# Value rows of the last 128 tokens summed on VectorE, and value tiles collected four at a time in PSUM

## The chip, the cores and the metric

The kernel runs on one core of a Trainium2 chip. The metric is the device time of one execution in microseconds; the median of three runs is given. Engines are named as in the profile: PE (TensorE matmul), PEld (its weight load), DVE (VectorE), ACT (ScalarE), POOL (GpSimd), SP (SyncE).

## The reference, cut to what matters

One transformer layer (differential attention, a pooling branch, gates) is followed by a mixture of 16,384 one-row experts. The change lies in the last part, the sum over value rows:

```python
def peer_block(h, w_q, sub_keys, u, v):
    ...                                        # 8 heads x 16 chosen experts = 128 for each token
    act = jax.nn.gelu(jnp.einsum('nd,nhkd->nhk', h, u[experts]), approximate=False)
    return jnp.einsum('nhk,nhkd->nd', (gate * act).astype(h.dtype), v[experts])
```

There are 576 tokens (512 of the prompt, 64 of the samples), `v` is 16,384 x 2048 in float32 (128 MB), and each token needs 128 rows of it. The result is added to `h` and normalized.

## The kernel before

Everything up to the value part stays as it is, but for small preparations. The value part treats three sets of tokens in two ways.

**Tokens 0 to 383 (`TV`), dense.** All of V is multiplied with a weight matrix that is zero where a token did not choose an expert. V is cut into 128 tiles of 128 experts x 2048 columns. SP loads a tile into one of two buffers `v_raw` (`load_v`, L566), ACT casts it to `v_hi` (`value_high`, L1116), DVE subtracts to get `v_lo` (`value_low`, L1712). Gates times activations are loaded by SP (`load_weights`, L569), multiplied by DVE (`weigh`, L1718), and split by ACT and DVE into `wx_hi` and `wx_lo` (L1123, L1724). PE works on pairs of tiles (loop at L2274): for each of 16 column blocks `d` it issues three products (hi·hi, hi·lo, lo·hi) for each of two tiles into one PSUM bank, six matmuls of 128x128 by 384 columns, and DVE adds the bank to `main` (`take_sum`, L1730). Four banks are used in turn: before block d, PE waits until DVE has taken block d-4 (L2286). There are 64 pairs and 1,024 `take_sum`.

**Tokens 384 to 575, gathered.** For these 192 tokens POOL gathers each token's 128 rows, with expert slots on the partitions (`gather_rows`, L748; 1 MB each). Four tokens make a batch; there are 48. PE multiplies a batch with a 128x32 weight tile per token, 16 float32 matmuls of 512 columns (`expert_sums`, L2231), before block d=4 of pairs 3 to 40 (32 batches) and 43 to 61 (16 batches). `e_rows` has eight buffers, two batches. The activations of tokens 384 to 447 (`N_CELL` = 64) are gathered too, one element per partition (`gather_cells`, L739); those of the last 128 tokens come from dot products on DVE (L1689).

**Order.** Each engine's program is written out by hand and runs in order; semaphores join them. DVE's order in a pair is `take_sum` for each d, with `value_low` after d=3 and 6, `weigh` after 8 and 9, `weight_low` after 11 and 12 (L1755 to L1771). POOL's loop (L780) waits for a batch's matmuls, weighs the batch two ahead, gathers its rows, and then gathers the cells four ahead. All gathers go out on POOL's own DMA queue (q0), all loads of SP on another (q1), and both run on the same 16 DMA engines.

Of the kernel before, what the change touches and what calls it, by code (L numbers as in the profile page):

```python
# [26 lines left out]
P = 128  # L27
# [45 lines left out]
N_CELL = TU - TV  # L73
U_RING = 3
# [31 lines left out]
def tokens(tb):  # L106
    return P if tb < TB - 1 else NS


def hybrid_step(nc, x_prompt, x_sample, cache_k, cache_v, state_pool, page_table, norm1_g, w_in, b_gate,  # L110
# [4 lines left out]
    with ctx:  # L115
# [55 lines left out]
        e_act = Region(masks_at, iota_at)("e_act", [P, N_SP])  # L171
        e_slot = Region(iota_at + P * 4, A_X)("e_slot", [P, PK], U32)
        e_cell = Region(iota_at + P * 4, A_X)("e_cell", [P, N_CELL], U32)
        e_row = Region(pages_at, A_X)("e_row", [P, N_SP], U32)
# [94 lines left out]
        v_raw = [r(f"v_raw{s}", [P, D]) for s in range(2)]  # L269
        wx_hi = [r(f"wx_hi{s}", [P, TV], R) for s in range(4)]  # L270
        wx_lo = [r(f"wx_lo{s}", [P, TV], R) for s in range(4)]
        e_rows = [r(f"e_rows{s}", [P, D]) for s in (5, 6)]
        g_back = [None, r("g_back1", [P, N_HALF, 2, GB // 2])]
        e_w = [r(f"e_w{s}", [P, COLS, QR]) for s in range(2)]
        r = Region(A_X, END)
        e_rows = [r("e_rows0", [P, D])] + e_rows
# [3 lines left out]
        e_gate = r("e_gate", [P, N_SP])  # L280
        r("spare", [P, N_SP])
        e_rows = e_rows[0:1] + [r(f"e_rows{s}", [P, D]) for s in range(1, 5)] + e_rows[1:]
        e_rows.append(Region(A_MAIN - D * 4, A_MAIN)("e_rows7", [P, D]))
        first_x = [Region(A_X + 2 * T * 4, back_at), Region(back_at + 4 * TV * 4 + 2 * N_SP * 4 + 3 * D * 4, END - 4096)]
        first_x = [[r(f"first_x{i}{j}", [P, TV], R) for j in range(2)] for i, r in enumerate(first_x)]
        first_hi = [nc.alloc_sbuf_tensor_at(f"first_hi{m}", [P, D], R, offset=BASE + back_at + 4 * TV * 4 + 2 * N_SP * 4 + 2 * m * D * 4) for m in range(2)]
        first_lo = nc.alloc_sbuf_tensor_at("first_lo", [P, D], R, offset=BASE + back_at + 4 * TV * 4 + 2 * N_SP * 4 + D * 4)
# [117 lines left out]
        V_RAW = [U_RAW[s] + 16 * NQ * N_U // 2 for s in range(2)]  # L405
        h_mm, H_MM, h_ev, H_EV = xr_mm, TB, xr_ev, 2 * TB
        dot_done, DOT = x_scaled, 2 * TB
        u_row_in, e_in = kp_in[0:U_RING], (vp_in, kp_in)
        U_IN = 16 * DB * PAGES // K_RING
        E_IN = [[U_IN] * COLS, [U_IN + 16 * len(range(j, N_SU, U_RING)) * (j < U_RING) for j in range(COLS)]]  # L410
        CELLS_IN = [16 * (2 + 8 + (8 if s < 2 else 0)) for s in range(4)]

        def batch_tokens(b):

            k = 0 if b < SP_BLOCKS[1][0] else 1
            first, nb, _ = SP_BLOCKS[k]
            return [COLS * first + nb * j + b - first for j in range(COLS)], b - first

        def value_parts(n):

            return first_hi[n] if n < 2 else v_hi[n % 4], first_lo if n == 0 else v_lo[n % 4]

        def weight_parts(n):

            return first_x[n] if n < 2 else (wx_hi[n % 4], wx_lo[n % 4])
# [63 lines left out]
        def _(sp):  # L489
# [76 lines left out]
            def load_v(n):  # L566
                sp.dma_start(v_raw[n % 2][:, :], v_tiles[:, n, :]).then_inc(raw_in[n % 2], 16)

            def load_weights(n):  # L569
                sp.dma_start(a_back[n % 2][:, :], gelu_dram[n][:, 0:TV]).then_inc(ag_in[n % 2], 16)  # L570
                if n % 2 == 0:
                    sp.dma_start(g_back[n // 2 % 2][:, :, :, :], gmat_dram[:, n // 2]).then_inc(ag_in[0], 16)
# [6 lines left out]
            sp.wait_ge(top_done, N_PQ + 5)  # L579
            for s in range(2):  # L580
                sp.wait_ge(a_out[s], 16)
                load_weights(s)
            sp.wait_ge(u_turn, 2 * N_U - 2)
            load_v(0)
            store_gelu(N_U - 3)
            sp.wait_ge(u_turn, 2 * N_U)
            load_v(1)
# [5 lines left out]
            for p in range(1, N_PAIR):  # L593
                for n in (2 * p, 2 * p + 1):
                    sp.wait_ge(v_lod, n - 1)
                    load_v(n)
                for s in range(2):
                    sp.wait_ge(a_out[s], 32 if p == 1 else 16 * N_U // 2)
                for n in (2 * p, 2 * p + 1):
                    sp.wait_ge(wx_lod, n - 1)  # L600
                    load_weights(n)
# [10 lines left out]
        def _(pool):  # L612
# [126 lines left out]
            def gather_cells(b):  # L739

                for t in batch_tokens(b)[0]:
                    if t >= N_CELL:
                        break
                    pool.indirect_dma_start(out=e_act[:, t:t + 1], out_offset=None, in_=gelu_cells,
                                            in_offset=bass.IndirectOffsetOnAxis(ap=e_cell[:, t:t + 1], axis=0)
                                            ).then_inc(back_in[b % 4], 16)

            def gather_rows(b):  # L748

                for j, t in enumerate(batch_tokens(b)[0]):  # L750
                    pool.indirect_dma_start(out=e_rows[b % 2 * COLS + j][:, :], out_offset=None, in_=v_rows,
                                            in_offset=bass.IndirectOffsetOnAxis(ap=e_row[:, t:t + 1], axis=0)
                                            ).then_inc(e_in[b % 2][j], 16)

            def weigh(b):

                ts_, c = batch_tokens(b)
                at = slice(ts_[0], ts_[-1] + 1, ts_[1] - ts_[0])
                if b < SP_BLOCKS[1][0]:
                    pool.wait_ge(back_in[b % 4], CELLS_IN[b % 4] + 32 * (b // 4 + 1))  # L760
                if b >= 2:
                    _, last = batch_tokens(b - 2)
                    g.memset(e_w[b % 2][:, :, last], 0.0).then_inc(e_wval, 1)
# [3 lines left out]
                g.tensor_tensor(e_w[b % 2][:, :, c], e_act[:, at], e_gate[:, at], ALU.mult).then_inc(e_wval, 1)  # L767

            pool.wait_ge(top_done, N_PQ + 5)
# [3 lines left out]
            for b in range(2):  # L773
                gather_rows(b)
            for b in range(4):
                gather_cells(b)
            pool.wait_ge(h_ev, H_EV + 6)
# [17 lines left out]
        def _(act):  # L795
# [320 lines left out]
            def value_high(n):  # L1116

                act.wait_ge(raw_in[n % 2], 16 * (n // 2 + 1) + V_RAW[n % 2])
                if n >= 4:
                    act.wait_ge(acc_ps, (n // 2 - 1) * KD)  # L1120
                a.copy(value_parts(n)[0][:, :], v_raw[n % 2][:, :]).then_inc(v_hid, 1)
# [1205 lines left out]
```

## Time and profile before

| | us |
|---|---|
| median of three runs | 4501.45 (4498.28 to 4503.62) |
| the profiled execution | 4504.14 |
| its span | 4502.4 |
| PE busy in the span | 4378.3 (97%) |
| DVE busy | 2908.6 (65%) |
| ACT busy | 1211.7 (27%) |
| POOL busy | 700.7 (16%) |
| value part: first and last matmul of L2260 | 3204.04 to about 4458.5 |

The profile sums instructions over one execution, so shares of busy time are means over stages with different limits. Durations of matmuls overlap: 337 ns is one matmul from start to end, while the next begins 0.17 us after it. Times "at" a point count from the start of the span.

### The profile page before, as it was taken

What the parts mean: (1) busy time and instruction counts of PE and PEld (TensorE: products, weight loads), DVE (VectorE), ACT (ScalarE), POOL (GpSimd) and SP (SyncE); (2) the same over time, 40 slices, a digit from 0 to 9 for tenths busy, and PEclk for the clock granted to TensorE, in tenths of its full rate; (3) what the DMA queues carried; (4) which work ended last, traced back from release to release, by engine and by line L of the source; (5) the groups of instructions that cost most, each with busy time, mean ns of one, the idle gap of its engine ahead of it and who ended that gap; (6) DMA issues with size and microseconds to landing.
All of it is one profiled execution on the core that took longest, in us unless ns stands there. A gap on an engine that the chain in (4) does not pass through costs nothing.

```text
span 4502.4 us, 69308 instructions
## 1 busy us (share of the span) xinstructions
PE 4378.3 (97%) x29448; PEld 4054.6 (90%) x29448; DVE 2908.6 (65%) x4670; ACT 1211.7 (27%) x1490; POOL 700.7 (16%) x744
## 2 busy tenths in 40 slices
PE   8999999999999989999999999999999999999997
PEld 7999889998899979888899999999988888898887
DVE  3232552322434366899998989898677777777777
ACT  3221442322212121223322222222222222222223
POOL 1010002331000000000111111111133333312220
PEclk9999999999999989999999999999999999999998
DMA  6333235775344533355899999999888888878872
GB/s 197 110 105 96 78 97 191 239 245 175 107 126 126 155 78 74 90 126 124 229 285 285 277 285 282 275 291 274 303 329 327 325 316 320 328 279 327 328 303 95
DMA packets 571731, 968.42 MB, mean 215 GB/s; under 512 B 140817, under 2 KB 402961, under 8 KB 512792
## 3 DMA queue, kind: packets, MB, share of 16 engines
q1 hardware_dynamic: 490128, 519.33, 40.7%
q0 software_dynamic: 75776, 434.18, 25.3%
q10 hardware_dynamic: 5520, 10.49, 0.8%
q8 instruction: 233, 3.82, 0.3%
q14 instruction: 74, 0.61, 0.0%
HBM read 873.63 MB, written 85.75 MB: 213 GB/s over the span
## 4 chain that ended last, share of the span: by engine, by line
PE 87%; DVE 9%; issue 1%; ACT 1%; DMA 1%; SPq 0%; ACTq 0%; DVEq 0%
PE pair L1838 28%; PE pair L2260 23%; PE pair L2179 21%; PE quad L2241 4%; PE quad L1838 2%; PE pair L2214 2%; DVE w_lo L1560 2%; PE pair L1802 1%; PE quad L1802 1%; DVE turned L1555 1%; PE quad L2009 1%; ACT w_hi L819 1%; PE pair L1874 1%; PE quad L2052 1%; DVE ts L1576 1%
## 5 line engine op out<-in xcount | busy, mean ns | idle before, releaser
L2179 PE MATMUL pair<-act_hi,w_hi 128*128 128x448 f32 x2048 | 758.8, 371 | 14.8 <-DVE w_lo L1560 14.8
L1733 DVE TENSOR_TENSOR main<-pair,main 128x384 f32<-128x384 f32 x1024 | 552.9, 553 | 323.3 <-PE pair L2260 322.8
L2179 PE MATMUL pair<-act_lo,w_hi 128*128 128x448 f32 x2048 | 749.7, 366 | 0.0
L2179 PE MATMUL pair<-act_hi,w_lo 128*128 128x448 f32 x2048 | 749.6, 366 | 0.0
L1838 PE MATMUL pair<-act_hi,w_hi 128*128 128x288 f32 x3264 | 719.4, 302 | 29.3 <-DVE act_lo L1265 12.3
L1205 DVE TENSOR_TENSOR w_lo<-w_raw,w_hi 128x2048 fp32r<-128x2048 f32 x103 | 236.1, 2293 | 747.0 <-ACT w_hi L819 747.0
L1838 PE MATMUL pair<-act_hi,w_lo 128*128 128x288 f32 x3264 | 702.8, 297 | 0.0
L1838 PE MATMUL pair<-act_lo,w_hi 128*128 128x288 f32 x3264 | 701.2, 297 | 0.0
L2260 PE MATMUL pair<-wx_hi,v_hi 128*128 128x384 f32 x2016 | 679.3, 337 | 1.6 <-DVE main L1733 1.6
L2260 PE MATMUL pair<-wx_hi,v_lo 128*128 128x384 f32 x2016 | 674.2, 334 | 0.0
L2260 PE MATMUL pair<-wx_lo,v_hi 128*128 128x384 f32 x2016 | 673.4, 334 | 0.0
L1838 PEld LDWEIGHTS pair<-act_hi,w_hi 128*128 128x128 f32 x3264 | 526.5, 190 | 67.7 <-issue 61.5
L1838 PEld LDWEIGHTS pair<-act_lo,w_hi 128*128 128x128 f32 x3264 | 528.8, 190 | 0.0
L1838 PEld LDWEIGHTS pair<-act_hi,w_lo 128*128 128x128 f32 x3264 | 528.7, 190 | 0.0
L819 ACT CAST w_hi<-w_raw 128x2048 fp32r<-128x2048 f32 x112 | 213.5, 1907 | 829.7 <-PE pair L1838 728.3
L2179 PEld LDWEIGHTS pair<-act_hi,w_hi 128*128 128x128 f32 x2048 | 385.8, 188 | 48.8 <-DVE w_lo L1560 15.0
L2260 PEld LDWEIGHTS pair<-wx_hi,v_hi 128*128 128x128 f32 x2016 | 378.3, 188 | 42.2 <-issue 40.2
L2179 PEld LDWEIGHTS pair<-act_hi,w_lo 128*128 128x128 f32 x2048 | 385.6, 188 | 31.1
L2179 PEld LDWEIGHTS pair<-act_lo,w_hi 128*128 128x128 f32 x2048 | 385.9, 188 | 29.7
L2260 PEld LDWEIGHTS pair<-wx_lo,v_hi 128*128 128x128 f32 x2016 | 378.4, 188 | 0.0
L2260 PEld LDWEIGHTS pair<-wx_hi,v_lo 128*128 128x128 f32 x2016 | 378.3, 188 | 0.0
L1560 DVE TENSOR_TENSOR w_lo<-turned,w_hi 128x1024 fp32r<-128x1024 f32 x256 | 309.0, 1207 | 103.9 <-ACT w_hi L1067 101.9
(323 smaller groups left out, 5206.8 us busy)
## 6 DMA issues: line engine op xcount, KB each, us to landing
w_raw<-in_peer_u_dram SPq DMA_DIRECT2D x512, 256.0 KB, 5.6
v_raw<-in_peer_v_dram SPq DMA_DIRECT2D x128, 1024.0 KB, 5.7
w_raw<-in_w_in_dram SPq DMA_DIRECT2D x64, 1024.0 KB, 6.8
gelu_dram<-tmp SPq DMA_DIRECT2D x128, 224.0 KB, 7.4
gmat_dram<-gmat SPq DMA_DIRECT2D x48, 512.0 KB, 11.2
a_back<-gelu_dram SPq DMA_DIRECT2D x128, 192.0 KB, 8.3
g_back<-gmat_dram SPq DMA_DIRECT2D x64, 384.0 KB, 9.5
w_raw<-in_w_out_dram SPq DMA_DIRECT2D x16, 1024.0 KB, 7.0
```

Source lines behind the costliest of these rows:

```text
L819: a.copy(w_hi[g % 2][:, :, :], w_raw[g % 2][:, :, :]).then_inc(hi_done, 1)
L1205: v.tensor_sub(w_lo[g % 2][:, :, :], w_raw[g % 2][:, :, :], w_hi[g % 2][:, :, :].bitcast(F)).then_inc(lo_done, 1)
L1555: v.transpose(turned[i][:, :, :].rearrange("p k (e c) -> p e k c", c=QR), raw[:, :, 8 * i:8 * i + 8, :]).then_inc(u_turn, 1)
L1560: v.tensor_sub(w_lo[s][:, 8 * i:8 * i + 8, :], turned[i][:, :, :], w_hi[s][:, 8 * i:8 * i + 8, :].bitcast(F)).then_inc(u_lo, 1)
L1576: link(*[v.max(out=ts[0:w, h, at:at + 8], in_=cand[0:w, h, :]) for h in range(PH)])
L1733: v.tensor_add(main[:, d, 0:TV], bank(d), main[:, d, 0:TV]).then_inc(acc_done, 1)
L1802: return nc.tensor.transpose(out, in_, ident[0:n, 0:n])
L1838: op = m_(pair[out][:, hf, 0:TH], w[:, k, :], x[:, k, hf * TH:(hf + 1) * TH], start=(starts and k == ks[0] and i == 0), stop=(ends and k = ...
L2179: op = m_(pair[0][:, n % 2, 0:TU], w[n % 2][:, k, :], x[:, k, 0:TU], start=(k == 0 and i == 0), stop=(k == KD - 1 and i == 2))
L2214: op = m_(pair[1][:, g % 2, n * PK:(n + 1) * PK], one_i[g % 2][:, n, :], gate_j[g % 2][:, n, :], start=True, stop=True)
L2241: op = m_(pair[2 + c // 2][quadrant(j), c % 2, :], e_w[b % 2][:, j, :], e_rows[b % 2 * COLS + j][:, c * 512:(c + 1) * 512], start=first, s ...
L2260: op = m_(bank(d), w[:, c], x[:, :], start=(start and t == terms[0]), stop=(stop and t == terms[-1]))
```

## The change

It has three parts.

1. **The last 128 tokens (448 to 575) leave PE.** Token on the partition, slot by slot: `gather_slot(i)` brings the i-th chosen row of all 128 tokens (1 MB, two buffers `s_rows`), and `add_slot(i)` on DVE does `s_sum = s_rows * weight + s_sum` over 2048 columns. The 128 sums are placed by the table `SUMS`: after d = 4, 7, 12 and 15 of groups 1 to 31, and after d=6 in groups 5, 12, 19 and 26. In the last group PE turns `s_sum` with 16 transposes and DVE adds the result to `main`.
2. **16 batches remain on PE** (tokens 384 to 447), before d=4 of groups 2, 3, 5, 6, 8, 9 ... 23, 24. `e_rows` has four buffers instead of eight, so the rows of batch b+1 are gathered after the matmuls of batch b. POOL then gathers the cells of batch b+2 and weighs that batch at once.
3. **PSUM collects four tiles.** The tiles are grouped (0, 1), then fours, and last (126, 127): 33 groups, 528 `take_sum`. V is loaded, cast and subtracted in halves of 1024 columns (three raw buffers of 512 KB, named by `V_HALF`). The high half (d 8 to 15) of a group's tiles is prepared in d 1 to 5 of the group itself, the low half of the next group's tiles in d 9 to 13. `wx_hi` and `wx_lo` have eight buffers.

The core of the diff (buffer addresses, names and the start of the stage are left out):

```diff
-SP_BLOCKS = ((0, 32, 3), (32, 16, 43))
-N_BATCH = sum(nb for _, nb, _ in SP_BLOCKS)
-SP_PAIR = {pair + i * 6 // 5: first + i for first, nb, pair in SP_BLOCKS for i in range(nb)}
-SP_LAST = {pair + (nb - 1) * 6 // 5: k for k, (_, nb, pair) in enumerate(SP_BLOCKS)}
+SP_N = 16
+SP_GROUP = [2 + 3 * b // 2 for b in range(SP_N)]
+SP_LAST = SP_GROUP[-1]
+V_GROUPS = [(0, 1)] + [tuple(range(n, min(n + 4, N_U))) for n in range(2, N_U, 4)]
+N_VG = len(V_GROUPS)
+V_GROUP = {n: g for g, ns in enumerate(V_GROUPS) for n in ns}
+V_HALF = [(0, 0), (0, 1), (1, 0), (1, 1)] + [(n, h) for ns in V_GROUPS[1:] for h in range(2) for n in ns]
+V_AT = {x: i for i, x in enumerate(V_HALF)}
+V_RAWS = 3
+SUMS = sorted([(g, d) for g in range(1, N_VG - 1) for d in (4, 7, 12, 15)] + [(g, 6) for g in (5, 12, 19, 26)])
+SUM_AT = {x: i for i, x in enumerate(SUMS)}
+BATCH_AFTER = {min(i for i, x in enumerate(SUMS) if x > (SP_GROUP[b], 4)) + 2: b for b in range(SP_N - 1)}
...
-            return [COLS * first + nb * j + b - first for j in range(COLS)], b - first
+            return [SP_N * j + b for j in range(COLS)]
...
+            def load_v(i):
+                if i >= V_RAWS:
+                    sp.wait_ge(v_lod, i - V_RAWS + 1)
+                n, half = V_HALF[i]
+                sp.dma_start(v_raw[i % V_RAWS][:, :], v_tiles[:, n, half * D // 2:(half + 1) * D // 2]).then_inc(v_in[i % V_RAWS], 16)
+
+            def load_weights(k):
+                if k:
+                    sp.wait_ge(wx_val, 2 * k)
+                for s in range(2):
+                    sp.wait_ge(a_out[s], 16 * (k + 1) if k < 2 else 16 * N_U // 2)
+                sp.dma_start(a_back[0][:, :], gelu_dram[2 * k][:, 0:TV]).then_inc(ag_in[0], 16)
+                sp.dma_start(g_back[k % 2][:, :, :, :], gmat_dram[:, k]).then_inc(ag_in[0], 16)
+                sp.dma_start(a_back[1][:, :], gelu_dram[2 * k + 1][:, 0:TV]).then_inc(ag_in[1], 16)
...
+            for g in range(1, N_VG):
+                if 2 + 2 * g < N_PAIR:
+                    load_weights(2 + 2 * g)
+                for n in V_GROUPS[g]:
+                    if V_AT[n, 1] + V_RAWS < len(V_HALF):
+                        load_v(V_AT[n, 1] + V_RAWS)
+                if 3 + 2 * g < N_PAIR:
+                    load_weights(3 + 2 * g)
+                for n in V_GROUPS[g + 1] if g + 1 < N_VG else ():
+                    if V_AT[n, 0] + V_RAWS < len(V_HALF):
+                        load_v(V_AT[n, 0] + V_RAWS)
```

```diff
+
+            def gather_slot(i):
+
+                pool.indirect_dma_start(out=s_rows[i % 2][:, :], out_offset=None, in_=v_rows,
+                                        in_offset=bass.IndirectOffsetOnAxis(ap=e_slot[:, i:i + 1], axis=0)
+                                        ).then_inc(s_in[i % 2], 16)
 
             def weigh(b):
+                pool.wait_ge(back_in[b % 4], CELLS_IN[b % 4] + 16 * COLS * (b // 4 + 1))
...
+            for i in range(2):
+                gather_slot(i)
+            gather_cells(0)
+            gather_rows(0)
+            gather_cells(1)
             for b in range(2):
                 weigh(b)
-            for b in range(N_BATCH):
-                pool.wait_ge(e_mm, b + 1)
-                if b + 2 < N_BATCH:
-                    weigh(b + 2)
-                    if b + 2 == SP_BLOCKS[0][1] + 1:
-                        pool.wait_ge(e_turned, 2)
-                    gather_rows(b + 2)
-                if b + 4 < N_BATCH:
-                    gather_cells(b + 4)
+            for i in range(2, PK + 2):
+                if i < PK:
+                    pool.wait_ge(s_done, S_DONE + i - 1)
+                    gather_slot(i)
+                if i in BATCH_AFTER:
+                    b = BATCH_AFTER[i]
+                    pool.wait_ge(e_mm, b + 1)
+                    gather_rows(b + 1)
+                    if b + 2 < SP_N:
+                        gather_cells(b + 2)
+                        weigh(b + 2)
```

```diff
+            def value_high(i):
+
+                n, half = V_HALF[i]
+                g, c = V_GROUP[n], slice(half * D // 2, (half + 1) * D // 2)
+                act.wait_ge(v_in[i % V_RAWS], 16 * (i // V_RAWS + 1) + V_IN)
+                if g >= 2:
+                    act.wait_ge(acc_ps, (g - 1) * KD + 8 * (half + 1))
+                a.copy(value_parts(n)[0][:, c], v_raw[i % V_RAWS][:, :]).then_inc(v_hid, 1)
...
+            for g in range(1, N_VG):
+                after = V_GROUPS[g + 1] if g + 1 < N_VG else ()
+                for n in V_GROUPS[g][0:3]:
+                    value_high(V_AT[n, 1])
+                for n in after[0:2]:
+                    weight_high(n)
+                for n in V_GROUPS[g][3:4]:
+                    value_high(V_AT[n, 1])
+                for n in after[0:3]:
+                    value_high(V_AT[n, 0])
+                for n in after[2:4]:
+                    weight_high(n)
+                for n in after[3:4]:
+                    value_high(V_AT[n, 0])
+                if g == SP_LAST:
+                    take_expert_sums()
```

```diff
+            def add_slot(i):
+
+                dve.wait_ge(s_in[i % 2], S_IN[i % 2] + 16 * (i // 2 + 1))
+                if i == 0:
+                    v.tensor_scalar(s_sum[:, :], s_rows[0][:, :], s_act[:, 0:1], None, ALU.mult).then_inc(s_done, 1)
+                else:
+                    dve.wait_ge(s_done, S_DONE + i)
+                    v.scalar_tensor_tensor(s_sum[:, :], s_rows[i % 2][:, :], s_act[:, i:i + 1], s_sum[:, :],
+                                           ALU.mult, ALU.add).then_inc(s_done, 1)
...
+            for g in range(1, N_VG):
+                after = V_GROUPS[g + 1] if g + 1 < N_VG else ()
                 for d in range(KD):
-                    if p == 0 and d == H_EARLY:
-                        dve.wait_ge(hT_back, 32)
-                    if p < N_PAIR - 1 or d < 12:
-                        take_sum(p, d)
-                    if p + 1 < N_PAIR:
-                        if d == 3:
-                            value_low(2 * p + 2)
-                        if d == 6:
-                            value_low(2 * p + 3)
-                        if d in (8, 9):
-                            weigh(2 * p + d - 6)
-                        if d in (11, 12):
-                            weight_low(2 * p + d - 9)
-                    if d == 13 and p - 1 in SP_LAST:
-                        add_expert_sums(SP_LAST[p - 1])
+                    if g < N_VG - 1 or d < 12:
+                        take_sum(g, d)
+                    if d in (0, 8):
+                        for n in after[d // 4:d // 4 + 2]:
+                            weigh(n)
+                    if d in (6, 14):
+                        for n in after[d // 8 * 2:d // 8 * 2 + 2]:
+                            weight_low(n)
+                    if d in (1, 2, 3, 5):
+                        i = (1, 2, 3, 5).index(d)
+                        for n in V_GROUPS[g][i:i + 1]:
+                            value_low(V_AT[n, 1])
+                    if d in (9, 10, 11, 13):
+                        i = (9, 10, 11, 13).index(d)
+                        for n in after[i:i + 1]:
+                            value_low(V_AT[n, 0])
+                    if (g, d) in SUM_AT:
+                        add_slot(SUM_AT[g, d])
+                    if (g, d) == (SP_LAST + 1, 11):
+                        add_expert_sums()
+                    if (g, d) == (N_VG - 1, 5):
+                        add_slot_sums()
```

```diff
-                    pe.wait_ge(e_added, 2)
                 for j in range(COLS):
-                    pe.wait_ge(e_in[b % 2][j], 16 * (b // 2 + 1) + E_IN[b % 2][j])
+                    pe.wait_ge(e_in[j], 16 * (b + 1) + U_IN)
...
+            for g, ns in enumerate(V_GROUPS):
+                if g:
+                    pe.wait_ge(v_lod, V_AT[ns[-1], 0] + 1)
+                    pe.wait_ge(wx_lod, ns[-1] + 1)
+                for d in range(0 if g else 4, KD):
+                    if d == 8:
+                        pe.wait_ge(v_lod, V_AT[ns[-1], 1] + 1)
+                    if d == 4 and g in SP_GROUP:
+                        expert_sums(SP_GROUP.index(g))
+                    if (g, d) == (SP_LAST + 1, 8):
+                        pe.wait_ge(e_taken, 2)
+                        turn_rows(e_rows[0])
+                    if (g, d) == (N_VG - 1, 2):
+                        pe.wait_ge(e_added, 2)
+                        pe.wait_ge(s_done, S_DONE + PK)
+                        turn_rows(s_sum)
+                    pe.wait_ge(acc_done, g * KD + d - 3)
+                    for n in ns:
+                        op = value_terms(d, n, (0, 1, 2), n == ns[0], n == ns[-1])
+                    op.then_inc(acc_ps, 1)
+            pe.wait_ge(acc_done, N_VG * KD)
```

## Rows read from the trace of the kernel before

**Rows 1.** The page, part 1: busy us, share of the span, instructions.
```profile
PE 4378.3 (97%) x29448; PEld 4054.6 (90%) x29448; DVE 2908.6 (65%) x4670; ACT 1211.7 (27%) x1490; POOL 700.7 (16%) x744
```
**Rows 2.** Groups by line, 3300 to 4502 us: busy us, mean ns | idle before.
```profile
L2260 PE MATMUL pair<-wx_hi,v_hi 128*128 128x384 f32 x1891 | 637.2, 337 | 0.0
...
L1733 DVE TENSOR_TENSOR main<-pair,main 128x384 f32<-128x384 f32 x947 | 512.1, 553 | 305.8 <-PE pair L2260 305.3
...
L1121 ACT CAST v_hi<-v_raw 128x2048 fp32r<-128x2048 f32 x116 | 220.4, 1912 | 253.3 <-PE pair L2260 214.1 <-DMA v_raw<-in_peer_v_dram 39.3
L2241 PE MATMUL quad<-e_rows,e_w 128*32 128x512 f32 x1472 | 167.5, 595 | 0.0
...
L1793 DVE SCALAR_TENSOR_TENSOR tmp<-main,gfc,rstd 128x576 f32<-128x576 f32 x16 | 12.6, 818 | 1.9 <-PE quad L1802 1.3
L1784 DVE TENSOR_TENSOR nf_sum<-nf_sum,nf_sq 128x576 f32<-128x576 f32 x15 | 11.3, 756 | 1.3
```
**Rows 3.** Busy time by stretch: PE, PEld, DVE, ACT, POOL, granted clock, DMA share, GB/s.
```profile
3216.00:3226.00 10.00, 10.00 (x51) 10.00 (x50) 8.84 (x15) 1.43 (x5) 0.00 (x0) 0.83 0.83 279
3400.00:3600.00 200.00, 200.00 (x1246) 174.05 (x1246) 144.85 (x220) 48.42 (x40) 70.75 (x72) 1.00 0.86 333
```
**Rows 4.** The chain that ended last, in order of time: start us, us, what.
```profile
3588.01 33.50 PE pair L2260 x192
...
3625.09 16.86 PE pair L2260 x96
...
3645.52 16.86 PE pair L2260 x96
```
**Rows 5.** Timeline of DVE: start us, us, line, operation [idle before].
```profile
3608.98 2.28 DVE L1716 TENSOR_TENSOR v_lo<-v_raw,v_hi 128x2048 fp32r<-128x2048 f32 x1
3611.18 1.01 DVE L1733 TENSOR_TENSOR main<-pair,main 128x384 f32<-128x384 f32 x2
3612.11 0.55 DVE L1722 TENSOR_TENSOR a_back<-a_back,g_back 128x384 f32<-128x384 f32 x1
3612.58 0.55 DVE L1733 TENSOR_TENSOR main<-pair,main 128x384 f32<-128x384 f32 x1
```
**Rows 6.** Timeline of POOL around one batch.
```profile
3625.59 0.96 POOL L751 DMA_INDIRECT e_rows<-in_peer_v_dram,e_row  x1
...
3633.76 0.95 POOL L744 DMA_INDIRECT e_act<-gelu_dram,e_cell  x1 [0.31 <-issue]
```
**Rows 7.** DMA of that batch, 3625.2 to 3645.6 us.
```profile
q0 software_dynamic: 635, 4.20, 53.6%
q1 hardware_dynamic: 706, 2.86, 37.5%
...
e_act<-gelu_dram,e_cell POOLq DMA_INDIRECT x2, 12.1
```
**Rows 8.** Timeline of POOL at the start of the stage.
```profile
3226.49 0.94 POOL L751 DMA_INDIRECT e_rows<-in_peer_v_dram,e_row  x1 [78.34 <-PE pair L2260]
...
3260.19 0.20 POOL L765 MEMSET e_w<- 128x128 f32 x1 [10.05 <-DMA e_act<-gelu_dram,e_cell]
```
**Rows 9.** DMA of 3300 to 4300 us: size, median us from issue to landing.
```profile
v_raw<-in_peer_v_dram SPq DMA_DIRECT2D x101, 1024.0 KB, 5.7
```
**Rows 10.** The tile e_rows over the same stretch.
```profile
DMA to landing us min/median/max: 6.5/8.0/16.8
```
**Rows 11.** Timeline of PE around a wait at the start of the stage.
```profile
3212.84 0.27 PE L1802 MATMUL quad<-ident,e_act 128*128 128x128 f32 x1
3215.57 0.70 PE L2260 MATMUL pair<-first_x,first_hi 128*128 128x384 f32 x2 [2.46 <-DVE main L1733]
3216.07 0.52 PE L2260 MATMUL pair<-first_x,first_lo 128*128 128x384 f32 x1
```

More of the change, by code:

```diff
@@ L73 @@
 N_CELL = TU - TV
+assert len(SUMS) == PK and SP_N * 4 == N_CELL
 U_RING = 3
@@ L268, in hybrid_step @@
         r = Region(A_RING, A_CONST)
[L269 to L272, printed above, removed]
+        v_raw = [r(f"v_raw{s}", [P, D // 2]) for s in range(V_RAWS)]
+        wx_hi = [r(f"wx_hi{s}", [P, TV], R) for s in range(8)]
+        lo_at = r.at - BASE
+        wx_lo = [r(f"wx_lo{s}", [P, TV], R) for s in range(8)]
+        wx = [Region(lo_at + s * TV * 4, A_CONST)(f"wx{s}", [P, TV]) for s in range(8)]
+        e_row3 = r("e_rows3", [P, D])
         g_back = [None, r("g_back1", [P, N_HALF, 2, GB // 2])]
         e_w = [r(f"e_w{s}", [P, COLS, QR]) for s in range(2)]
+        s_sum = Region(A_MAIN - D * 4, A_MAIN)("s_sum", [P, D])
+        first_lo = [None, Region(A_MAIN - D * 4, A_MAIN)("first_lo1", [P, D], R)]
         r = Region(A_X, END)
-        e_rows = [r("e_rows0", [P, D])] + e_rows
+        e_rows = [r("e_rows0", [P, D])]
         back_at = r.at - BASE
@@ L279, in hybrid_step @@
         g_back[0] = r("g_back0", [P, N_HALF, 2, GB // 2])
[L280 to L287, printed above, removed]
+        e_gate = r("e_gate", [P, N_CELL])
+        e_cell = r("e_cell", [P, N_CELL], U32)
+        rows_at = r.at - BASE
+        e_rows += [r(f"e_rows{s}", [P, D]) for s in (1, 2)] + [e_row3]
+        s_rows = [r(f"s_rows{s}", [P, D]) for s in range(2)]
+        r = Region(A_X + 2 * T * 4, back_at)
+        first_x = [[r(f"first_x0{j}", [P, TV], R) for j in range(2)]]
+        first_wx = [Region(A_X + 2 * T * 4 + TV * 4, back_at)("first_wx0", [P, TV])]
+        r = Region(rows_at, END - 4096)
+        first_hi = [r("first_hi0", [P, D], R)]
+        first_lo[0] = r("first_lo0", [P, D], R)
+        first_hi.append(r("first_hi1", [P, D], R))
+        first_wx.append(Region(r.at - BASE + TV * 4, END)("first_wx1", [P, TV]))
+        first_x.append([r(f"first_x1{j}", [P, TV], R) for j in range(2)])
         r = Region(back_at, END)
@@ L592, in _ @@
             sp.wait_ge(a_done, N_U)
[L593 to L601, printed above, removed]
+            load_v(3)
+            load_weights(1)
+            for i in (4, 5, 6):
+                load_v(i)
+            load_weights(2)
+            for i in (7, 8, 9):
+                load_v(i)
+            load_weights(3)
+            load_v(10)
+            for g in range(1, N_VG):
[9 more added lines that the diff above has]
+                        load_v(V_AT[n, 0] + V_RAWS)
             for n in range(4):
@@ L766, in weigh @@
                     pool.wait_ge(e_wval, 2 * b + 1)
[L767 to L769 removed]
+                g.tensor_tensor(e_w[b % 2][:, :, b], e_act[:, b::SP_N], e_gate[:, b::SP_N], ALU.mult).then_inc(e_wval, 1)
+            pool.wait_ge(top_done, N_PQ + 4)
             pool.wait_ge(acc_ps, KD)
@@ L1745, in add_expert_sums, with add_slot_sums @@
                     op.then_inc(e_added, 1)
+            def add_slot_sums():
+                for i in range(2):
+                    dve.wait_ge(e_turned, 2 + i + 1)
+                    ps, ks = turned_x(pair[2 + i], P), slice(8 * i, 8 * i + 8)
+                    v.tensor_add(main[:, ks, T - NS:T], ps[:, :, 0:NS], main[:, ks, T - NS:T])
+                    v.tensor_add(main[:, ks, TU:T - NS], ps[:, :, NS:P], main[:, ks, TU:T - NS]).then_inc(e_added, 1)
             for m in range(2):
```

200 lines of the change are left out of this document (87 added, 113 removed).

## The prediction

> **What bounds the kernel now.** The page's busy shares come first: PE is busy for 97% of the span and DVE for 65% [rows 1]. Shares are means over stages, so the next view is the stretch of the value part: from 3400 to 3600 us PE is busy all the time at the full clock, DVE 72%, ACT 24%, and the 16 DMA engines 86% at 333 GB/s [rows 3]. The groups say with what: the matmuls of L2260 (this row for each of three products), the 32-column float32 matmuls of L2241, and on DVE above all `take_sum` [rows 2]. DVE's idle time before `take_sum` is 305.8 us, 305.3 of it put down to PE [rows 2]: DVE waits for PE, not the reverse. The chain in order of time gives the rhythm: two pairs, one of them with a batch, take 3625.09 - 3588.01 = 37.08 us, and one pair with a batch 3645.52 - 3625.09 = 20.43 us [rows 4]. So a bare pair takes 16.65 us (1.04 per block d) and a batch adds 3.78 us. Only PE is on the chain.
>
> **What the change takes from PE.** The matmuls of the dense part stay as they are; PSUM collects twelve instead of six, so a block lasts 2.08 us and a group of four tiles 33.3 us. Of 48 batches 16 stay: 32 x 3.78 = 121.0 us leave PE. The transposes of the sums are 32 before and after, and one transpose of activations goes; I cost this at nothing.
>
> **Does DVE still fit beside PE?** Durations overlap by a little, so I take distances between starts: `value_low` 2.20 us (3608.98 to 3611.18), a 384-column operation 0.47 us (3612.11 to 3612.58) [rows 5]. Per group of four tiles: 16 `take_sum` 7.5, 8 `weigh` and `weight_low` 3.7, 8 halves of `value_low` at about 1.13 (half the columns, the same start cost) 9.0, and 4 `add_slot`. No row shows that operation at 2048 columns; scalar_tensor_tensor takes 818 ns against 756 for a plain addition at 576 columns [rows 2], so between 2.20 and 2.20 x 818/756 = 2.38; I take 2.2, because the difference looks like a start cost, not one per column: 8.8. The sum is 29.0 us of 33.3. DVE's share rises from 72% to 87% although `take_sum` takes 7.5 instead of 15 us of the same work. It keeps up on average, and `take_sum` may lag by three blocks (6.2 us) before PE waits. But two other deadlines are closer. The last high half of V is subtracted after d=5, and PE needs it before d=8: if `add_slot` at d=4 starts at its planned place, that is ready 1.7 us early. The last `weight_low` of a group comes after d=14 and is ready some 0.4 us before PE's next group. So a late `add_slot` at d=4 costs PE whatever exceeds 1.7 us.
>
> **When are the gathered rows there?** This is the main added cost. In the trace one batch of four rows (4 MB) and two cell gathers goes out from 3625.59; the last cell gather is issued at 3633.76 and lands 12.1 us later, 20.3 us after the first issue [rows 6, 7]. Both queues share the engines then, q0 53.6% and q1 37.5% [rows 7]. At the start of the stage eight rows and eight cell gathers take 3260.19 - 3226.49 = 33.7 us [rows 8]. Hence 3.35 us for each further MB: five rows take about 23.7 us. In the new kernel POOL, at the place of a batch, issues one slot row, four batch rows and four cell gathers and then stands still until the cells have landed, because `weigh(b+2)` follows directly. Behind it, on the same engine, is the gather of the slot row for d=4 of the next group. Before the change the cells had been gathered a batch earlier and nobody waited for them.
>
> Clock of one group g with a batch, from its start: PE ends d=7 at 8 x 2.08 + 3.8 = 20.4; DVE takes it and adds the slot, 23.2; POOL issues there. The cells land at 23.2 + 23.7 = 46.9, POOL gathers the slot at 47.5, and it lands 8.0 later (the median of these gathers [rows 10]) at 55.5. Batches are followed alternately by a group without one (after batches 1, 3 ... 13: seven times) and by a group with one (after batches 0, 2 ... 14: eight times).
> - Followed by none: group g ends at 37.1, DVE wants the slot of d=4 at 48.2. It comes 7.3 late, less 1.7 of room: PE stands 5.6 us. A standing PE also loses clock: after a gap of 2.46 us the next matmuls take 0.52 instead of 0.33 us [rows 11], and the next 10 us ran at a granted 0.83 [rows 3], that is 1.7 us lost. 7 x 7.3 = 51 us. Bounds: POOL free already after 20.3 and a landing in the quickest 6.5 [rows 10] give 0.7 each, 5 us in all. For the slow end SP's own loads count: 5.2 MB of rows and 3.8 MB that SP loads meanwhile (six halves of V and the weights of a pair), at 4.20 + 2.86 MB in 20.4 us [rows 7], are 26 us; with the landing 8.0 that is 9.6 each with the clock, 67 us.
> - Followed by one: the four batch rows, in the same queue, are there at about 46.9; PE wants them at 37.1 + 8.3 = 45.4. It stands 1.5 us, and the slot that follows is about 0.3 late: 8 x 1.8 = 14 us. Bounds: 0 and, with 26 us and the clock, 8 x 5.5 = 44 us.
> - Start of the stage: POOL's first request is six rows and eight cell gathers, 20.3 + 2 x 3.35 = 27 us, then the slot for d=12 of group 1, wanted at 27.7, lands at 27 + 0.6 + 8.0 = 35.6; with 0.5 of room PE stands 7.4, plus clock 1.7. Preparing four half tiles and four weights in the 16.6 us of group 0 may be 2 late. 11 us (0 to 15).
> - Groups 5, 12, 19, 26 place a third sum at d=6. The row for d=7 is gathered only when the sum of d=4 is done and lands 3.5 us late on DVE, of which d=14 still feels about 1.5: 6 us (0 to 14).
> - The loads of V in halves: 1 MB lands in 5.7 us in the median [rows 9]; a half must land in 6.5 us at d=13 (below). Cost 0, up to 10.
>
> **The sum.** 4504.1 (the profiled execution) - 121 + 51 + 14 + 11 + 6 = 4465. The median of the runs is 2.7 us under the profiled execution, so **4462**. With all lower bounds the costs are 5 us (4386 on the median's scale), with all upper ones 150 us (4531).
>
> The landing times carry this, and a rule of the skill gives others. The Trainium skill, DMA: Bandwidth & Descriptors, section "Anatomy of one DMA — SWDGE (gpsimd) path", fits a transfer at 2.0 us plus its bytes over 436 GB/s. By that estimate five rows are there in 14 us, POOL is free long before it is needed, and only the 121 us remain. The trace does not agree where both queues work: 4 MB of rows took 20 us, not 12.
>
> **The rivals.**
> - *The rows are there in time* (chance 0.15). If SP's loads fall in the pauses of q0, five rows could take the time of four, 20.3 us or less, and the landings 6.5: no wait at d=4 exceeds its room. For it: in a batch's period the two queues have 91% between them, so a tenth is free [rows 7]. Against it: the DMA engines are at 86% already [rows 3], the bytes stay the same, and the time shrinks. Costs 5 to 25 us: 4386 to 4405. This is also what the skill's fit above would give.
> - *Slower: the halves of V come late* (chance 0.2). Place: `value_low` after d=13, the last of the next group. Its buffer comes free with the sum after d=9 (22.7 us after the start of a bare group), its load stands behind two weight loads and a `g_back` in q1, ACT casts it (about 1.0, half of the 1.9 that the row L1121 of the groups gives [rows 2]), and the last `weight_low` follows. It must land 6.5 us after issue. A whole tile lands in 5.7 in the median [rows 9], rows of q0 in 8.0 and up to 16.8 [rows 10]. At 9.0, every group is 2.5 us late: 31 x 2.5 = 78 us on top of the 82 above, 4540. From 1.6 us late per group (a landing after 8.1 us) the change is slower than before by more than 9 us. For it: three small buffers instead of two large ones, and busier DMA. Against: a half is half the bytes.
> - *The costs just eat the gain* (chance 0.12): the waits at d=4 at their slow end with the other terms (67 + 44 + 11 + 6 = 128, less 121), 4492 to 4511.
> - *The change doesn't do what it says*: that is excluded for PE, whose 512 matmuls are gone from its program.
>
> **How the numbers follow.** My forecast, waits behind the batch of gathers that cost 30 to 112 us, has 0.53: 4411 to 4492 by its own range. A measurement of this kernel can tell about 0.2%, 9 us, from no change. Forecast and first rival are faster: 0.68. Same: 0.12. Slower: 0.20. The range for 8 in 10 leaves out the quick end of the first rival and the far half of the second: 4398 to 4525.
>
> **What would show it.** Right: L2241 with a third of its instructions; DVE near 87% in the middle of the stage; PE's gaps about 7 us long at d=8 of groups 4, 7, 10 ... 22 with the releaser DVE `v_lo`, before it DVE `s_sum` waiting for the DMA `s_rows`, and POOL's `e_w` waiting for the DMA `e_act`; from group 25 on bare groups of 33.3 us. After each gap a few matmuls at 0.52 us. Wrong: `s_rows` landing without DVE waiting (first rival), or gaps in every group, also after group 25, with `v_raw` as the releaser of ACT (second). If `add_slot` took over 3 us, DVE itself would be the bound, and no landing time would matter.

## The result, and the profile after

| | before | after |
|---|---|---|
| median of four runs, us | 4502.3 | 4559.27 (4553.33 to 4564.21) |
| ratio | | 1.0128, 95% interval 1.011 to 1.0145 |
| span of the profiled execution | 4502.4 | 4556.9 |
| PE busy in it | 4378.3 (97%) | 4298.1 (94%) |

The kernel became 57 us slower; 40 us faster had been forecast. PE did lose the work: L2337, which answers to L2241 of [rows 2], has a third of its instructions. The page's first part:

```profile
PE 4298.1 (94%) x28423; PEld 4058.2 (89%) x28423; DVE 2952.4 (65%) x4428; ACT 1221.2 (27%) x1614; POOL 671.0 (15%) x680
```

Busy time by stretch, in the middle of the value part and after its last batch (columns as in [rows 3], where PE was busy all the time):

```profile
3400.00:3600.00 200.00, 176.28 (x1023) 163.82 (x1022) 141.69 (x169) 46.82 (x57) 57.98 (x52) 0.93 0.80 300
4300.00:4400.00 100.00, 97.08 (x559) 96.49 (x558) 89.76 (x107) 29.19 (x35) 12.28 (x13) 1.00 0.84 298
```
In the middle PE is idle for 12% and has a granted clock of 0.93. DVE is at 71%, far from the 87% forecast, and the DMA engines at 80%, less than before: nothing is full. After the last batch PE is at 97% with the full clock and DVE at 90%, about the list that was added up. So in the steady part of the stage the time is lost where batches are; a smaller loss at the start of the stage comes on top (see "Why the prediction was wrong").

The groups of lines (columns as in [rows 2]):

```profile
L1794 DVE SCALAR_TENSOR_TENSOR s_sum<-s_rows,s_act,s_sum 128x2048 f32<-128x2048 f32 x122 | 285.8, 2343 | 12.6 <-DMA s_rows<-in_peer_v_dram,e_slot 12.6
L1773 DVE TENSOR_TENSOR v_lo<-v_raw,v_hi 128x1024 fp32r<-128x1024 f32 x233 | 283.4, 1216 | 128.3 <-ACT v_hi L1168 128.3
...
L1168 ACT CAST v_hi<-v_raw 128x1024 fp32r<-128x1024 f32 x233 | 240.8, 1050 | 882.0 <-DMA v_raw<-in_peer_v_dram 671.6 <-PE pair L2355 210.1
...
L2337 PE MATMUL quad<-e_rows,e_w 128*32 128x512 f32 x480 | 54.6, 595 | 0.0
```
`add_slot` takes 2343 ns, `value_low` of a half 1216. From start to start they are 2.25 us (3601.86 to 3604.11 on DVE's timeline) and 1.13 (3630.72 to 3631.85), inside what had been set down (2.20 to 2.38, and 1.13). ACT's cast of V, L1168, has 671.6 us of idle time that end with a load of V; the row of L1121 in [rows 2], which answers to it, had 39.3. And the slot rows, which the forecast feared, cost DVE 12.6 us in all.

The chain in order of time shows one gap from end to end (start us, us, what):

```profile
3582.41 8.55 PE pair L2355 x48
...
3595.70 1.14 DVE v_lo L1773
...
3596.86 13.48 DMA v_raw<-in_peer_v_dram
...
3610.36 1.05 ACT v_hi L1168
...
3611.44 1.24 DVE v_lo L1773
...
3614.17 44.52 PE pair L2355 x240
```
PE works until 3590.96. Its next matmul of this chain starts at 3614.17, after: `value_low` of the next group's first tile (3595.70, d=9), which frees a raw buffer; the load into it, 13.48 us; cast; and `value_low` at d=13. Only then come the last `weight_low` and the next group. A chain does not say how long PE stood (it also worked on the rest of its group meanwhile). PE's timeline does, for this place:

```profile
3614.17 0.66 PE L2355 MATMUL pair<-wx_hi,v_hi 128*128 128x384 f32 x1 [6.58 <-issue]
```
and the stretch after it (columns as in [rows 3]):

```profile
3616.00:3618.00 2.00, 2.00 (x8) 2.00 (x7) 0.80 (x1) 1.39 (x2) 1.37 (x3) 0.50 0.22 78
```
It stood 6.58 us, and the granted clock then was 0.50, the lower of its two levels. What that costs is on the chain one gap earlier: the first 48 matmuls of the group (from 3568.66) take 10.18 us, the 48 after its batch 8.55. The view of waits has 22 idle stretches of PE with 124 us, the longest 10.2:

```profile
ACT v_hi L1168 <- DMA v_raw<-in_peer_v_dram: 671.6, 144, 17.4
...
DVE v_lo L1773 <- ACT v_hi L1168: 128.3, 26, 10.4
PE pair L2355 <- issue: 124.1, 22, 10.2
...
DVE s_sum L1794 <- DMA s_rows<-in_peer_v_dram,e_slot: 12.6, 4, 6.4
```
The chain restarts after such gaps at 3442.70, 3488.28 and 3568.66. From the first to the last are three groups with two batches: 125.96 us, where 3 x 33.3 + 2 x 3.78 = 107.5 were due by the prices of [rows 4], so 9.2 us for each of the two gaps between them, its slow clock included. From group 2 to group 24 the chain holds 14 loads of V of 13.3 us or more (13 of them up to 14.9, one 17.1), one for each of POOL's 15 requests but one; at that one, near 3740 us, it goes over a cell gather of 6.60 and a slot row of 9.20 instead, which is the forecast's path.

The two gaps are not the dearest. Measured from `take_sum` of block d=8 to that of the next group on DVE's timeline, the fifteen stretches after a request are 8.8 to 12.4 us over their price (33.3, and 3.78 for a batch in them), 156 us together; the other stretches up to group 31 are over it by 19 us in all.

What happens beside the load is on POOL's timeline:

```profile
3594.07 0.94 POOL L798 DMA_INDIRECT s_rows<-in_peer_v_dram,e_slot  x1 [5.30 <-DVE s_sum L1794]
...
3607.86 0.95 POOL L785 DMA_INDIRECT e_act<-gelu_dram,e_cell  x1 [0.31 <-issue]
3616.45 0.11 POOL L806 MEMSET e_w<- 128x4 f32 x1 [7.64 <-DMA e_act<-gelu_dram,e_cell]
```
Its nine gathers go out from 3594.07; the load of V is issued at 3596.84, into that burst. And the DMA engines do not share evenly. Rows of queues (packets, MB, share of 16 engines), first of the kernel before, 3634.5 to 3638.5, when rows and V (8 KB per partition) were under way:

```profile
q1 hardware_dynamic: 108, 0.88, 52.2%
q0 software_dynamic: 113, 0.82, 48.5%
```
and of the kernel after, 3601 to 3605 us (q1 has weights in pieces of 1.5 and 3 KB):

```profile
q0 software_dynamic: 180, 1.34, 79.5%
q1 hardware_dynamic: 181, 0.36, 22.9%
```
and 3606 to 3613 us (q1 has halves of V, 4 KB per partition):

```profile
q0 software_dynamic: 268, 1.97, 67.4%
q1 hardware_dynamic: 263, 0.98, 35.0%
```
Equal numbers of packets in all three, but bytes 1:1 before and 2:1 or nearly 4:1 after. A packet is one piece of a row here. So in these stretches the queues are served alternately, packet by packet; in others of the same burst the counts differ (154 of q0 and 246 of q1 from 3597 to 3601 us). This agrees with the Trainium skill, DMA: Bandwidth & Descriptors, section "Queues, rings and completion order", by which an engine goes round the queues packet by packet. It gives halves of V 0.14 MB per us beside a burst, where whole tiles had 0.22.

### The profile page after: what moved, and what is told of

It is laid out like the page before. It is cut to its first block, busy times and chain, and to the rows that moved or that the text cites. A ratio compares the mean times of both kernels' runs of the same rounds, so it can differ in the third digit from the quotient of the medians.

```text
span 4556.9 us, 67360 instructions
## 1 busy us (share of the span) xinstructions
PE 4298.1 (94%) x28423; PEld 4058.2 (89%) x28423; DVE 2952.4 (65%) x4428; ACT 1221.2 (27%) x1614; POOL 671.0 (15%) x680
## 4 chain that ended last, share of the span: by engine, by line
PE 77%; DVE 12%; DMA 7%; issue 2%; ACT 2%; SPq 0%; POOL 0%; ACTq 0%; DVEq 0%
PE pair L1937 28%; PE pair L2278 21%; PE pair L2355 16%; DMA v_raw<-in_peer_v_dram 5%; PE quad L1937 2%; PE pair L2313 2%; DVE w_lo L1615 2%; PE pair L1901 1%; PE quad L2337 1%; PE quad L1901 1%; DVE s_sum L1794 1%; DVE turned L1610 1%; DVE v_lo L1773 1%; PE quad L2108 1%; ACT w_hi L864 1%
## 5 line engine op out<-in xcount | busy, mean ns | idle before, releaser
L2355 PE MATMUL pair<-wx_hi,v_hi 128*128 128x384 f32 x2016 | 696.4, 345 | 136.9 <-issue 124.1
L2355 PE MATMUL pair<-wx_lo,v_hi 128*128 128x384 f32 x2016 | 690.0, 342 | 0.0
L2355 PE MATMUL pair<-wx_hi,v_lo 128*128 128x384 f32 x2016 | 689.3, 342 | 0.0
L2355 PEld LDWEIGHTS pair<-wx_hi,v_hi 128*128 128x128 f32 x2016 | 391.6, 194 | 158.2 <-issue 148.7
L1168 ACT CAST v_hi<-v_raw 128x1024 fp32r<-128x1024 f32 x252 | 260.5, 1050 | 937.0 <-DMA v_raw<-in_peer_v_dram 715.5
L1800 DVE TENSOR_TENSOR main<-pair,main 128x384 f32<-128x384 f32 x528 | 291.6, 554 | 187.8 <-PE pair L2355 187.6
L1773 DVE TENSOR_TENSOR v_lo<-v_raw,v_hi 128x1024 fp32r<-128x1024 f32 x252 | 306.5, 1216 | 137.2 <-ACT v_hi L1168 137.2
L2355 PEld LDWEIGHTS pair<-wx_lo,v_hi 128*128 128x128 f32 x2016 | 391.6, 194 | 0.0
## 6 DMA issues: line engine op xcount, KB each, us to landing
gmat_dram<-gmat SPq DMA_DIRECT2D x48, 512.0 KB, 12.4
```

Of the source, the lines that this page charges most:

```text
L1168: a.copy(value_parts(n)[0][:, c], v_raw[i % V_RAWS][:, :]).then_inc(v_hid, 1)
L1773: v.tensor_sub(lo[:, c], v_raw[i % V_RAWS][:, :], hi[:, c].bitcast(F)).then_inc(v_lod, 1)
L1800: v.tensor_add(main[:, d, 0:TV], bank(d), main[:, d, 0:TV]).then_inc(acc_done, 1)
L2355: op = m_(bank(d), w[:, c], x[:, :], start=(start and t == terms[0]), stop=(stop and t == terms[-1]))
```

## The experiments

All were compared with the kernel before on the same chip (its single time there lay between 4498 and 4513), and their differences to it are what is read: the changed kernel stands at +57. All but the last are single runs; repeated runs of one changed kernel lay within 11 us. Theory P is the forecast's mechanism (POOL stands behind its cell gathers, so slot rows come late), theory Q is the load of V beside the burst, theory D is a VectorE that is too slow.

**No batch rows** (they are gathered for the first batch only, so the value rows of tokens 384 to 447 are made of the first batch's rows):

```diff
-                    gather_rows(b + 1)
...
-                    pe.wait_ge(e_in[j], 16 * (b + 1) + U_IN)
+                    pe.wait_ge(e_in[j], 16 + U_IN)
```

> Leaves out the gathers of batch rows after the first batch (60 of the 64 rows of tokens 384 to 447); the matmuls run on the first batch's rows. Theory Q (the half of V for d=13 comes late because POOL's burst of five rows takes the DMA engines from SP's queue): the fifteen gaps of about 11.7 us go; 4504 - 121 + 10 to 25 = 4393 to 4408. Theory P (the forecast: slot rows late behind the standing POOL): the same. Theory D (VectorE itself is too slow for its list): it stays above 4530.

4428.8 against 4513.1: -84, 141 us less than the changed kernel. Theory D falls: DVE's list is the same. P and Q both expected this, so it shows that the batch rows cost these 141 us and not yet by which path. Of the 156 us in the fifteen stretches 13 are left. 37 us of the 121 stay away even so, more than expected.

**POOL does not stand** (the batch is weighed two sums later):

```diff
-                        weigh(b + 2)
+                if i - 2 in BATCH_AFTER and BATCH_AFTER[i - 2] + 2 < SP_N:
+                    weigh(BATCH_AFTER[i - 2] + 2)
```

> POOL weighs batch b+2 two sums later, so it does not stand behind the cell gathers. Theory Q: the burst is the same, the gaps stay: 4545 to 4562. Theory P: the waits behind the standing POOL go, 4460 to 4490.

4566.9 against 4513.1: +54. The waits for V are all there (695.7 us on ACT). As the only change, P is worth nothing that one run can show.

**The half of V ahead of the weights** in SP's queue:

```diff
-                if 3 + 2 * g < N_PAIR:
-                    load_weights(3 + 2 * g)
                 for n in V_GROUPS[g + 1] if g + 1 < N_VG else ():
                     if V_AT[n, 0] + V_RAWS < len(V_HALF):
                         load_v(V_AT[n, 0] + V_RAWS)
+                    if n == V_GROUPS[g + 1][0] and 3 + 2 * g < N_PAIR:
+                        load_weights(3 + 2 * g)
```

> SP issues the last low half of V (for d=13) before the weights of the second pair, not after them. Theory Q: in a burst the weights ahead of it cost it about 5 us, so the load lands in 8 instead of 13.5 us and each gap of 11.7 shrinks to 5 to 7: 4556 - 15 x 6 = 4466 (4440 to 4500). Theory P and theory D: no change, 4550 to 4562.

4500.3 against 4513.1: -13, so 70 us less than the changed kernel, though at the slow end of what was expected. The place in the queue matters: P had expected no change. The chain shows what is late next:

```profile
3589.29 16.90 DMA a_back<-gelu_dram
...
3606.21 0.56 DVE wx L1778
...
3609.39 10.55 DMA v_raw<-in_peer_v_dram
3619.96 1.05 ACT v_hi L1168
```
The weights took 16.9 us, their product held up DVE, and then a half of V took 10.55.

**The kernel before with V in halves of 4 KB:**

```diff
-                sp.dma_start(v_raw[n % 2][:, :], v_tiles[:, n, :]).then_inc(raw_in[n % 2], 16)
+                for half in range(2):
+                    c = slice(half * D // 2, (half + 1) * D // 2)
+                    sp.dma_start(v_raw[n % 2][:, c], v_tiles[:, n, c]).then_inc(raw_in[n % 2], 16)
...
```

> The kernel before, with each tile of V loaded by two DMAs of 1024 columns (4 KB per partition) instead of one of 2048. Theory Q (the engines alternate between the queues by packet, so 4 KB pieces get half the bytes of 8 KB rows): beside the row gathers SP's queue moves about 140 GB/s against 280, where before both had 205 to 210; a tile takes 9 us or more in a batch's pair; the time stays within 10 us of 4502, because a tile of V has a whole pair of room there. Rival (bytes are shared evenly whatever their size): both near 205 GB/s, landing times as before.

4510.8 against 4513.1: -2. Queues from 3640 to 3644 us, with rows and halves of V under way:

```profile
q0 software_dynamic: 165, 1.20, 70.8%
q1 hardware_dynamic: 122, 0.50, 30.1%
```
1.20 MB against 0.50, where whole tiles had even shares (SP's queue has fewer packets here, 122 against 165, so it had pauses too): halves get the smaller share. V does come later: from 3300 to 4250 us ACT waits 134.3 us for it, where whole tiles had 35.5. The kernel before had the room to bear it.

**Rows in pieces of 4 KB** (each gather twice, 1024 columns; the half rows are of other experts, so the value rows of tokens 384 to 575 are made of those):

```diff
-                pool.indirect_dma_start(out=s_rows[i % 2][:, :], out_offset=None, in_=v_rows,
...
+                for c in (slice(0, D // 2), slice(D // 2, D)):
+                    pool.indirect_dma_start(out=s_rows[i % 2][:, c], out_offset=None, in_=v_halves,
...
```

> Every gathered row (batch and slot) is fetched by two gathers of 1024 columns, 4 KB per partition, with the same bytes; the index is left as it is, so it fetches half rows of other experts. Theory Q: packets of equal size, so in a burst both queues move about 210 GB/s instead of 270 and 139; the late half of V lands in 9 to 11 us instead of 13.5 and a gap of 11.7 shrinks to 7 to 9: 4556 - 15 x 3.5 = about 4505 (4480 to 4530). Rival (the size of a piece does not matter, only the bytes waiting): no gain, and POOL issues twice as many gathers: 4550 to 4580.

4589.0 against 4498.2: +91, worse. Of the shares it says what was expected. From 3575 to 3579 us, with 4 KB pieces in both queues:

```profile
q1 hardware_dynamic: 228, 0.85, 52.1%
q0 software_dynamic: 220, 0.79, 49.7%
```
The slowest load of V from 3300 to 4250 us lands after 11.4 us, in the changed kernel after 18.8, and DVE's wait for the cast of V falls from 125.1 to 36.1 us (in part, perhaps, because a burst is spread over a longer time). Of the time it says nothing: with 14 gathers for a burst POOL itself is on the chain (the one longest share between 3560 and 3700 us after PE's matmuls is the issue of `e_rows`, 20.8%), and `s_rows` is what DVE waits for, 143.1 us. What the even share alone is worth in time stays open.

**Rows two and two, and spread over the stage.** In both, a table says behind which sum after a batch (0 is the one where all went out before) each gather and the weighing go. The first kernel uses `ONE` for all batches; the second, "spread", uses `ONE` where the next group has a batch and `TWO` elsewhere, and moves the batches so that they reach to the end of the stage. The tables of the second:

```diff
-SP_GROUP = [2 + 3 * b // 2 for b in range(SP_N)]
+SP_GROUP = [2 + 28 * b // 15 for b in range(SP_N)]
...
+ONE, TWO = [(0, 'row', 0), (0, 'row', 1), (1, 'row', 2), (1, 'row', 3), (2, 'cells', 0), (4, 'weigh', 0)], [(0, 'row', 0), (1, 'row', 1), (2, 'cells', 0), (3, 'row', 2), (4, 'row', 3), (4, 'weigh', 0)]
...
```

> The rows of a batch are gathered two and two behind two sums, its cells behind the third, weighed behind the fifth; the same bytes. Theory Q: instead of five rows three stand in the queue at once, so the half of V for d=13 is 3 to 4 us late instead of 7: 4556 - 15 x 6 = 4466 (4430 to 4500). Rival (only the sum of the bytes counts, DMA is simply full): no change, 4545 to 4565.

> As e6, but the 16 batches are spread over groups 2 to 30, almost always two groups apart, and their rows go out one by one behind the sums. Theory Q: never more than two rows in the queue at once, the half of V is at most 1 us late: 4504 - 121 + 15 to 35 = 4398 to 4418. Theory D (VectorE too slow): above 4500.

4530.9 and 4526.9 against 4498.2: +33 and +29. Both missed what Q expected, and the first its rival as well; the second is where D would have it, but D had fallen with 4428.8 for the same list of DVE. That the burst alone is the cause was too simple. The chain of the second shows two halves late in one group (d=13 and then d=5), shorter than after the burst:

```profile
3580.48 8.50 DMA v_raw<-in_peer_v_dram
...
3600.34 6.85 DMA v_raw<-in_peer_v_dram
...
3616.68 9.83 DMA v_raw<-in_peer_v_dram
...
3658.49 9.24 DMA v_raw<-in_peer_v_dram
```
Two rows (a batch's and a slot's) and the weights beside it are enough: 6.9 to 9.8 us, and the room is 6.5. Spreading the bytes only spreads the gaps. Theory Q2 followed: the fault is that three raw buffers leave a load no time.

**Four raw buffers instead of three** (room from one `g_back` where there were two, `e_w` moved; the start of SP's list one load further):

```diff
-V_RAWS = 3
+V_RAWS = 4
...
-        g_back = [None, r("g_back1", [P, N_HALF, 2, GB // 2])]
...
-        g_back[0] = r("g_back0", [P, N_HALF, 2, GB // 2])
+        g_back = [r("g_back0", [P, N_HALF, 2, GB // 2])] * 2
...
-            load_v(10)
+            load_v(11)
```

The half for d=13 is then loaded after the `value_low` at d=5 instead of d=9, ahead of the weights. Alone, and with each of the three edits of POOL's order above:

> One more raw buffer for halves of V (four instead of three), nothing else in the order but that each load is issued one half earlier; the room comes from using one g_back where two were. Theory Q2 (each half must land 6.5 us after its buffer comes free, and the queues cannot do that beside gathers; with four buffers a half has 16 us): the gaps for V go; what stays are waits for slot rows behind the standing POOL (theory P), 4400 to 4460. Rival B (the DMA engines simply have too many bytes, whatever the order): above 4510.

> As e8, and POOL weighs batch b+2 two sums later, as in e2. Theory P (with V on time, the standing POOL is the next wait): 15 to 50 us below e8. If P is wrong at this point too: equal to e8 within 10 us.

> As e8, with the rows of a batch two and two as in e6. Theory Q2 with P: the burst is gone as well, 4395 to 4430, no worse than e11. Rival B: above 4510.

> As e8, with the batches over groups 2 to 30 and their rows one by one as in e7. Theory Q2: the fewest bytes per group, 4390 to 4415, the best of the four. Rival B: near e7, 4510 to 4530.

| against the kernel before, us | three raw buffers | four |
|---|---|---|
| POOL's order as in the change | +57 | -14 (4494.1 against 4508.3) |
| weighed later | +54 | -78 (4430.6) |
| two and two, weighed later | +33 | -47 (4461.2) |
| spread over the stage, weighed later | +29 | -82 (4426.3) |

The fourth buffer takes 71 us off, though 4494 is above the 4460 that was expected at most. It changes two things at once, the lead of the load and its place ahead of the weights; the place alone (V ahead of the weights, with three buffers) had taken 70. What differs is what is left: from 3250 to 4400 us DVE waits 72.8 us for the cast of V there and 29.9 with four buffers, 127.8 in the changed kernel, and for slot rows 31.4, 92.5 and 12.6. V first with three buffers and later weighing was not run, so that the lead was needed for what follows is not shown.

Then the order of POOL decides: weighing later is worth 3 us with three buffers and 64 with four. With four, the chain is the one of the forecast (part of it, start us, us, what):

```profile
3540.01 0.94 POOL s_rows L797
...
3548.05 2.92 POOL e_act L784
...
3554.28 8.94 DMA e_act<-gelu_dram,e_cell
3563.27 0.11 POOL e_w L805
...
3564.26 9.64 DMA s_rows<-in_peer_v_dram,e_slot
3573.93 2.35 DVE s_sum L1793
...
3576.67 1.22 DVE v_lo L1772
```
POOL issues at 3540.01, is free at 3563.27 (23.3 us later; forecast 23.7), the slot row is there at 3573.90 (33.9; forecast 32.3), DVE adds it, and PE gets its V. Two and two was expected to be no worse than weighing later and is 31 us worse; PE waits there for `e_rows`, 35.1 us in 8 waits, because the last two rows go out a sum later (that this is the reason was not tested). The spread kernel has PE busy and the full clock nearly throughout, from 3400 to 3600 us:

```profile
3400.00:3600.00 200.00, 199.39 (x1176) 191.92 (x1165) 171.97 (x204) 54.98 (x66) 54.83 (x54) 1.00 0.90 347
```
DVE is at 86% there, about the 87% that the forecast had added up, and the DMA engines at 90%.

**The last one timed:**

> The kernel of e10, timed against the kernel before in five rounds. Both theories of the other runs expect what its single run gave: 82 us under the kernel before on the same chip, a ratio of 0.982 (0.979 to 0.985), and so about 3% under the changed kernel's 1.0128.

4416.0 (4413.1 to 4424.3) against 4502.8, ratio 0.9809 (0.9796 to 0.9823). It beats both kernels, and the changed one by 3%.

## Why the prediction was wrong

- **PE's 121 us: right.** Groups that wait for nothing take 33.3 us after the change too (66.80 for two on the chain of the last kernel, from 3467.52), and a batch 3.8 more. That kernel reaches 87 of the 121 (4502.8 - 4416.0).
- **DVE's list: right.** 2.25 us from start to start for `add_slot`, 86 to 90% busy where nothing holds it up. It takes 62 ns more than a subtraction of the same width (2343 and 2281), as it had at 576 columns (818 and 756): a start cost, as assumed. DVE was never the bound.
- **POOL's standing and the late slot row: right in mechanism, but hidden in the changed kernel.** Its price was 51 + 14 = 65 us; with four buffers, taking it away gives 64. That the sum fits so well is luck: measured from d=8 to d=8, 37 us go from the seven groups after a batch that have none themselves (51 forecast), and 31 from the other stretches (14 forecast). In the changed kernel DVE already stood at d=13 for V when the slot row was late, so the two waits lay over each other: DVE waited 12.6 us for slot rows instead of 7 x 7.3 = 51, and weighing later gained 3.
- **The failed step is "The loads of V in halves ... Cost 0, up to 10".** It gave the load 6.5 us of room and set 5.7 us against it, the median over all loads of the kernel before, as if half the bytes made it only quicker. Wanted was the time of this one load: behind the weights of a pair, in a queue that gets one packet for each packet of 8 KB of a burst issued 3 us earlier. It took 13.3 to 14.9, so it was 7 to 8 us late; with the clock and the third sums in four groups the fifteen stretches lost 8.8 to 12.4 us each, 156 us for a term of 0 to 10.
- **The second rival** named the place, d=13, and had a chance of 0.2. Of its sign one half came true, `v_raw` as the releaser of ACT; the other, gaps in every group, did not: the groups after the last batch have none. Its 4540 lies near 4559 by luck. It is 78 us of late halves (2.5 in each of 31 groups) on top of 82 for the other terms; measured are 156 in fifteen stretches and little on top, since the waits for slot rows lay under them.
- **The range** ended at 4525, since all upper bounds together gave 4531 with this term at 10.
- **The rest.** 156 - 121 = 35 us is not yet 57; the other 22 are not of this load. Of these, the first stretch of the stage (group 0 to 1) is 7.5 us over its price and the one after it 1.0 (the start had been priced at 11). In the best kernel, where V is on time, 34 to 39 of the 121 us stay away in its two sets of runs. There the four stretches with a third sum (groups 5, 12, 19 and 26) are over their price by 13 to 15 us together (6 forecast, 14 at most), and those of groups 3 and 16, which have a batch right behind a group with one, by some 7 each. What remains was not taken apart.

## What to carry to other kernels

A load's time is that of the moment when it is issued: look up what stands ahead of it in its queue and what the other queue does then, not its median. When a tile is cut into halves, its buffers give half the lead, and its shorter pieces get a smaller share of the DMA engines beside long ones; count both. Waits that lie over each other hide each other's price: an edit that gains nothing alone can be worth 64 us once the other wait is gone.

## What the runs showed of the hardware

- In the stretches shown where both queues had work, they were served packet for packet: 0.88 MB against 0.82 with 8 KB pieces in both, 0.85 against 0.79 with 4 KB in both, 1.97 against 0.98 with 8 KB and 4 KB, 1.34 against 0.36 with 8 KB and mostly pieces of 1.5 and 3 KB. The engines moved 410 to 425 GB/s together each time.
- After PE had stood 6.58 us its granted clock was 0.50 (3616 to 3618 us). After the gap before that one, 48 matmuls of 384 columns took 10.18 us instead of 8.55.
- On GpSimd one gather is 0.94 us of work and the next starts 1.24 us after it (3594.07, 3595.31); in a burst the fourth to sixth take 1.78, 1.77 and 2.92 us.
- Five rows of 1 MB with four cell gathers took 22.4 us from the first issue until POOL went on (3594.07 to 3616.45), while SP's queue was at work too. The estimate for the five rows by the fit in the Trainium skill, DMA: Bandwidth & Descriptors, section "Anatomy of one DMA — SWDGE (gpsimd) path", is 14 us; the trace does not agree.
